# First expert block gathered by index, gate pieces moved around the turns, and separate waits in the expert tails

## The reference, cut to what matters

```python
x = x + parallel_mixer(rms_norm(x, g_mix), ...)
x = x + memory_cross_attention(rms_norm(x, g_xattn), rms_norm(mem, g_mem), ...)
x = x + hier_moe(rms_norm(x, g_moe), ...)              # expert width 512
x = rms_norm(x, g_final)
for l in range(2):
    x = _layernorm(alpha * x + _token_mixer(x, ...), ln1_g, ln1_b)    # alpha = 4 ** 0.25
    x = _layernorm(alpha * x + _hier_moe(x, ...), ln2_g, ln2_b)       # expert width 256

# hier_moe: top 1 of 4 groups by softmax, top 2 of its 8 experts
#   y = (silu(xb @ w_gate[e]) * (xb @ w_up[e])) @ w_down[e]
#   out[t] = sum of w * y over the token's two experts

# _token_mixer: z = x @ w_in, split in parts
y_a = _mla(...)                    # softmax attention
y_b = _stick_breaking(...)         # log sigmoid, suffix sums
y_c = _conformer_conv(...)
y_d = _forgetting_attention(...)   # logits + c[t] - c[s], c = cumsum(log_sigmoid(f))
gates = sigmoid(gate_logits + b_gate).reshape(b, s, 4, d)
merged = sum(einsum('bsnc,ncd->bsnd', ys, w_branch) * gates, axis=2)
return merged @ w_o
```

## Time and profile before

| | us |
|---|---|
| median of 3 runs | 2870.16 |
| lowest, highest | 2865.46, 2873.40 |
| the profiled execution | 2872.35 |
| span of its trace | 2870.5 |

### The profile page before, as it was taken

How to read it: one execution, slowest core, us unless ns; L and a number is a source line. 1 busy time by engine, 2 the same in 40 slices (tenths; PEclk the granted TensorE clock), 3 DMA queues, 4 the chain that set the end, 5 groups by cost and what they waited for, 6 DMA issues and landing times. The chain is left out here.

```text
span 2870.5 us, 50656 instructions
## 1 busy us (share of the span) xinstructions
PE 2500.0 (87%) x18285; PEld 1976.6 (69%) x18286; DVE 1364.5 (48%) x2996; ACT 926.8 (32%) x1739; POOL 363.6 (13%) x694
## 2 busy tenths in 40 slices
PE   7987799898888887999899889985989989989882
PEld 6976698764445446876677877764877767877662
DVE  6466335421111126735653744446744744654345
ACT  3534333221111114335442323324334633223222
POOL 1000000021212220000000034431000000014332
PEclk9998899699999998999999879997999989969997
DMA  4201325499999944132122579994222222469994
GB/s 150 74 1 60 103 89 208 174 408 405 409 405 412 395 199 164 45 83 56 47 64 61 201 278 365 386 374 144 78 64 56 56 55 79 179 240 386 375 390 159
DMA packets 209353, 565.32 MB, mean 197 GB/s; under 512 B 26768, under 2 KB 170768, under 8 KB 184640
## 3 DMA queue, kind: packets, MB, share of 16 engines
q1 hardware_dynamic: 191296, 538.74, 50.5%
q0 software_dynamic: 17920, 24.73, 2.6%
HBM read 559.69 MB, written 36.18 MB: 208 GB/s over the span
## 5 line engine op out<-in xcount | busy, mean ns | idle before, releaser
L989 PE MATMUL ps<-m_gate_up,e_xT 128*64 128x256 f32 x1088 | 270.7, 412 | 62.8 <-DMA m_gate_up<-in_w_gate_up 45.1
L989 PEld LDWEIGHTS ps<-r_gate_up,e_xT 128*64 128x64 f32 x2272 | 261.4, 142 | 86.9 <-issue 53.0
L989 PE MATMUL ps<-r_gate_up,e_xT 128*64 128x128 f32 x2272 | 273.5, 281 | 37.8 <-DMA r_gate_up<-in_w_exp_gate_up 24.8
L1159 DVE TENSOR_TENSOR e_hid<-e_silu,ps 64x128 f32<-64x128 f32 (+1 forms) x210 | 70.3, 335 | 473.6 <-ACT e_silu L1033 463.4
L989 PEld LDWEIGHTS ps<-m_gate_up,e_xT 128*64 128x64 f32 x1088 | 160.4, 149 | 175.2 <-issue 111.3
L1033 ACT ACTIVATE e_silu<-ps 64x128 f32<-64x128 f32 (+1 forms) x210 | 63.6, 303 | 660.0 <-PE ps L991 655.4
L991 PE MATMUL ps<-r_gate_up,e_xT 128*64 128x128 f32 x2272 | 273.7, 281 | 0.0
L991 PE MATMUL ps<-m_gate_up,e_xT 128*64 128x256 f32 x1088 | 270.7, 412 | 0.0
L991 PEld LDWEIGHTS ps<-r_gate_up,e_xT 128*64 128x64 f32 x2272 | 261.4, 142 | 0.0
L1242 POOL COPY e_tokcur<-e_tokcol 64x1 uint32 (+1 forms) x112 | 22.5, 201 | 1752.2 <-DVE e_tokcol L1119 1723.1
L2417 PE MATMUL ps<-t_hT,t1a_t1g_w 128*128 128x512 f32 x768 | 199.7, 411 | 4.8 <-PEq L54 2.4
(11 more groups left out here) (666 smaller groups left out, 4880.5 us busy)
## 6 DMA issues: line engine op xcount, KB each, us to landing
m_gate_up<-in_w_gate_up SPq DMA_DIRECT2D x32, 4096.0 KB
r_gate_up<-in_w_exp_gate_up SPq DMA_DIRECT2D x64, 2048.0 KB
m_down<-in_w_down SPq DMA_DIRECT2D x32, 2048.0 KB
r_down<-in_w_exp_down SPq DMA_DIRECT2D x64, 1024.0 KB
t0a_t0g_raw<-in_w_in SPq DMA_DIRECT2D x32, 512.0 KB, 3.8
t1a_t1g_raw<-in_w_in SPq DMA_DIRECT2D x32, 512.0 KB, 3.8
mixw_raw<-in_w_in SPq DMA_DIRECT2D x10, 1024.0 KB
xaw_raw<-in_w_kv_x SPq DMA_DIRECT2D x8, 1024.0 KB
```

The source lines that it names most:

```text
L989: nc.tensor.matmul(ps_gu[q][0:SLOTS], xT[:, c, :], ring.gu[s][:, 0, c, span], start=c == 0, stop=c == DC - 1)
L1159: vec.tensor_tensor(hid[SLOTS:P, q], silu[SLOTS:P, q], ps_gu[q][SLOTS:P], ALU.mult).then_inc(hid_ready, 1)
```

## The change

- **Expert stages.** The first block goes the way of the others: gather(0, 0), copy to `gathered`, `turn()`. The one-hot table and `first_rows` are gone. POOL clears `landing` with a memset. gather(2, 0) is issued only when DVE has copied block 0. DVE does all four `grow` ahead of the wait for block 0's rows. The number of full pairs joins the table; the counts of tokens have their own PSUM bank.
- **POOL's loop.** The index column of a store is copied before the wait for `y`, after a wait for the store two blocks back.
- **Tails.** DVE waits for the stores of the real blocks; SP does not wait for the store of e2's empty block. The norm's rows are loaded while the experts run. In e2's tail (x + mean) * gain is formed by DVE while ACT works on the root, and one more operation multiplies by the factor and adds the bias; ACT's rescale is gone there; the last tile is stored in two halves.
- **Gate pieces.** At u = 8, 16, 24 the projection (u, 2) and the half gate (u + 1, 0) change places; each of mx, sx, fx gets one half gate behind its transposes; the merged stage fs gets projection (16, 2). ma takes 26 pieces, sa 23, fa 22, `finish` 21.
- **fs, L2334, fr** become one stage; the log sigmoids are computed at the head of sa.

```diff
-def turn_split(nc, name, k, tiles, src, dst, n, factor=None):
+def turn_split(nc, name, k, tiles, src, dst, n, factor=None, pe_side=None):
...
                 turned.pe(pe)
+                if pe_side is not None:
+                    pe_side(pe)
...
+                if act_head is not None:
+                    act_head(act, link)
...
+                if norm.out is not None:
+                    read = sp.value_load(table[0:1, 1, (TURNS - 1) * RING + 2:(TURNS - 1) * RING + 3], min_val=1, max_val=MAX_BLOCKS)
+                    sp.wait_ge(gu_ready, read * 2)
+                    for n in range(2):
+                        sp.dma_start(norm_rows[:, n], norm.rows[n].partition_broadcast(P)).then_inc(norm_rows_landed, 16)
+                n_pairs, n_full = pairs_of_blocks(sp), full_pairs(sp)
+                sp.wait_ge(y_stored[1], n_full * 16 + 32)
+                sp.wait_ge(y_stored[0], n_pairs * 16 + 32)
...
-                    if norm.out is not None and t == 0:
-                        for n in range(2):
-                            sp.dma_start(norm_rows[:, n], norm.rows[n].partition_broadcast(P)).then_inc(norm_rows_landed, 16)
...
-                def first_rows():
-
-                    pe.wait_ge(first_pos_ready, 1)
-                    for c in range(DC):
-                        for t in range(TT):
-                            last = nc.tensor.matmul(ps_turn[:, c * SLOTS:(c + 1) * SLOTS], x[:, t, c * P:(c + 1) * P],
-                                                    first_pos[:, t, :], start=t == 0, stop=t == TT - 1)
-                    last.then_inc(turned, 1)
-
-                first_rows()
-                pe.wait_ge(table_ready, 2)
+                pe.wait_ge(rows_staged, 1)
+                turn()
...
-                nc.scalar.activation(landing[:].rearrange("p n d -> p (n d)"), k["ones"][0:SLOTS, 0:1].to_broadcast([SLOTS, 2 * D]),
-                                     ACT.Identity, scale=0.0).then_inc(landing_cleared, 1)
...
-                link(vec.tensor_scalar(near[:], in_block, 0.0, None, ALU.is_equal))
-                if not scaled:
-                    for j in range(2):
-                        last = vec.tensor_tensor(near[:, j * TT:(j + 1) * TT], near[:, j * TT:(j + 1) * TT], router.r[:, 2], ALU.mult)
-                    link(last)
-                link(vec.tensor_tensor(near_pos, at_pos.rearrange("p j t s -> p (j t) s"), cols(near[:], SLOTS), ALU.mult))
-                vec.tensor_tensor(first_pos, near_pos[:, 0:TT], near_pos[:, TT:], ALU.add).then_inc(first_pos_ready, 1)
...
-                    def grow(t):
-                        return vec.scalar_tensor_tensor(x[:, t, :], x[:, t, :], alpha, finish_rows[:, 0], ALU.mult, ALU.mult)
+                    dve.wait_ge(finish_landed, 32)
+                    for t in range(TT):
+                        last = vec.scalar_tensor_tensor(x[:, t, :], x[:, t, :], alpha, finish_rows[:, 0], ALU.mult, ALU.mult)
+                    link(last)
...
-                dve.sem_inc(rows_staged, 1)
+                dve.wait_ge(rows_gathered[0], 16)
+                vec.tensor_copy(gathered[:], landing[:, 0]).then_inc(rows_staged, 1)
                 turn_copy(1)
-                if finish is not None:
-                    dve.wait_ge(finish_landed, 32)
-                    for t in range(2):
-                        last = grow(t)
-                    link(last)
...
-                dve.wait_ge(choicecur_ready, g)
-                dve.wait_ge(y_stored[0], (g + 4) // 2 * 16)
-                dve.wait_ge(y_stored[1], (g + 3) // 2 * 16)
+                dve.wait_ge(y_stored[0], (g + 5) // 2 * 16)
+                dve.wait_ge(y_stored[1], (g + 4) // 2 * 16)
...
+                def shift(t):
+                    if norm.out is not None:
+                        if t == 0:
+                            dve.wait_ge(norm_rows_landed, 32)
+                        dve.wait_ge(centred, t + 1)
+                        vec.scalar_tensor_tensor(shifted[:, t, :], x[:, t, :], added[:, 1, t:t + 1], norm_rows[:, 0], ALU.add,
+                                                 ALU.mult).then_inc(grown, 1)
+
                 def last_factors(t):
                     if norm.out is not None:
-                        dve.wait_ge(normed, t + 1)
-                        if t == 0:
-                            dve.wait_ge(norm_rows_landed, 32)
-                        link(vec.tensor_tensor(x[:, t, :], x[:, t, :], norm_rows[:, 0], ALU.mult))
-                        vec.tensor_tensor(x[:, t, :], x[:, t, :], norm_rows[:, 1], ALU.add).then_inc(finished, 1)
+                        dve.wait_ge(grown, t + 1)
+                        form = (added[:, 4, t:t + 1], norm_rows[:, 1], ALU.mult, ALU.add)
+                        if t < TT - 1:
+                            vec.scalar_tensor_tensor(x[:, t, :], shifted[:, t, :], *form).then_inc(finished, 1)
+                        else:
+                            for h in range(2):
+                                at = slice(h * 512, (h + 1) * 512)
+                                vec.scalar_tensor_tensor(x[:, t, at], shifted[:, t, at], form[0], norm_rows[:, 1, at], ALU.mult,
+                                                         ALU.add).then_inc(half_finished, 1)
...
-                    for t in range(2, TT):
-                        last = grow(t)
-                    link(last)
...
                     pool.wait_ge(choicecur_ready, n + 1)
+                    pool.wait_ge(y_copied, n + 2)
                     step_aside()
...
+                nc.gpsimd.memset(landing[:], 0.0).then_inc(landing_cleared, 1)
                 pool.wait_ge(landing_cleared, 1)
                 pool.wait_ge(tokcol_ready, 1)
-                pool.sem_inc(tokcur_ready, 1)
-                gather(1, 1)
-                gather(2, 0)
-                nc.gpsimd.dma_start(spare_dram[4:5], ident[0:1, 0:SLOTS]).then_inc(rows_gathered[0], 16)
+                for n in range(2):
+                    gather(n, n)
                 for n in range(4):
                     nc.gpsimd.dma_start(spare_dram[n:n + 1], ident[0:1, 0:SLOTS]).then_inc(y_stored[n % 2], 16)
                 pool.wait_ge(choicecol_ready, 1)
+                pool.wait_ge(rows_staged, 1)
+                gather(2, 0)
...
-                        pool.wait_ge(y_copied, n + 2)
+                        pool.wait_ge(y_stored[p], pair * 16 + 32)
+                        step_aside(1)
...
+                        def _(pe):
+                            nc.tensor.matmul(sums, k["upto"][:], logs[:, 3], start=True, stop=False)
+                            for u in range(1, TT):
+                                last = nc.tensor.matmul(sums[:, u:TT], k["ones"][:], logs[:, 3, 0:TT - u],
+                                                        start=False, stop=u == TT - 1)
+                            last.then_inc(summed, 1)
+                            branches.pe_steps(pe, branches.next["pe"] + 1)
+                            pe.wait_ge(r_ready, 1)
+                            for j in range(4):
+                                for t in range(TT):
+                                    last = nc.tensor.matmul(ps[:, j, t * P:(t + 1) * P], r[:, t, j:j + 1].to_broadcast([P, P]),
+                                                            k["ident"][:], start=True, stop=True)
+                                last.then_inc(full, 1)
...
+        self.order = [(u, part) for u in range(self.units) for part in range(3)]
+        for u in range(DC, self.units, DC):
+            self.order[3 * u + 2:3 * u + 4] = [(u + 1, 0), (u, 2)]
...
-        return 3 * self.target + min(24, max(0, int((step + 1) * 24 / steps)))
+        span = 3 * self.target + 26 - self.start
+        return self.start + min(span, max(0, int((step + 1) * span / steps)))
...
-        turn_split(self.nc, name, self.k, TT, lambda t, c: ys[:, t, c * P:(c + 1) * P], self.yT, 2)
+        turn_split(self.nc, name, self.k, TT, lambda t, c: ys[:, t, c * P:(c + 1) * P], self.yT, 2,
+                   pe_side=lambda pe: self.pe_steps(pe, self.next["pe"] + 1))
```

202 lines of the change are left out of this document (87 added, 115 removed).

## The result

The changed kernel takes 2851.39 us (median of 6 runs, 2849.44 to 2858.35) beside 2869.19 for the one before (6 runs, 2863.6 to 2873.4) on the same chip: a ratio of 0.9949, interval 0.9934 to 0.9964. It is faster by 18 us, inside the range, but less than half of the 41 between 2870 and the 2829 that I gave as the likeliest. The profiled executions agree: 2852.16 (span 2849.7) against 2872.35 (2870.5).

A forecast was written before the change was run, and what follows sets the result against it. Bounds: PE in the attentions, standing DMA engines at the heads of e0 and e1, a chain in e2's tail. Heads, tails and mixers (-22) sum to -41.9 from 2872.35, less 2.2 to the median: 2829 us, range 2812 to 2852.

The forecast's parts named there:

- Heads: Start of the expert stages: gathering block 0 early gives -5.7 us in e0, -4.5 in e1, -0.3 in e2.
- A gather under full DMA load took 3.8 us: Heads: time from gather start to the copy waiting for it, read from an earlier row and used for block 0's landing.
- R3: Rival, heads: gather 0 queues behind the ring's loads, landing about 16 us late; 2867 us; chance 0.03, with R1 0.02.
- Each us by which the first expert is done earlier moves the whole stage: Heads of e0 and e1: the DMA engines stand until the first refill, so an earlier first expert shortens the stage equally.
- The memset ... Nothing: Heads: POOL's memset is done before `tokcol` comes, and the extra counting matmul falls on standing engines; 0 us.
- End of e2: Tail of e2: earlier read back and first add -6.2, with the stall and norm terms -8.3 us; bounds -5 and -11.
- stall -3.6, forms +1.7, half store -0.3: e2's tail behind the first add: second-tile stall goes, DVE's new norm forms cost 1.7 us, halved last store gives 0.3.
- Mixers: t0 and t1: -15.9 us each at full clock, about 0 at half clock in the turns; 0.7 of the way, -11 each.
- PE is the time there: Attentions: PE sets their length, so three half gates and one projection taken out gain all 10.8 us per mixer.
- R2: Rival, attentions: other waits come once PE's load falls, so only half of 10.8 is gained; 2840 us; chance 0.17.
- R1: Rival, mixer turns: clock stays low, gates take 4.9 us, mixers gain 0 instead of -11 each; 2851 us; chance 0.15.
- Merged fs: Each mixer, from sx's transposes to fa's first product: 15.7 us becomes 11.3 at full clock, -4.4.

The follow-up runs named there:

- h1: Changed kernel, but SP holds the ring's late loads in each expert stage until block 0's rows are staged; 2862.56 us in one execution.
- v1: Changed kernel, but only 2 of 8 MB of late loads in e0 and 4 of 10 in e1 go at once, the rest after block 0's rows; 2847.89 us.
- a1: Changed kernel, but ACT clears `landing` instead of POOL's memset, and the final norm has the earlier operations and whole stores; 2845.89 us in one execution.
- t1: As a run, not the mixer: changed kernel, but SP waits again for e2's empty block's store before reading back; 2856.15 us in one execution.
- h3: Changed kernel with the earlier head back: block 0 by one-hot matmuls, earlier order of gathers and grows, ACT clearing `landing`; 2850.57 us, ratio 0.9937.
- p1: Changed kernel with PE's half gates of units 9 to 16 cut from 12 matmuls to 4 (result wrong); sa takes 85.1 and 81.8 us.
- p2: Changed kernel with ACT's and DVE's gate operations of units 9 to 16 cut from 512 to 8 columns; sa 81.6 us, or 83.1 with a lower-clock stretch.
- m1: Changed kernel with the gate pieces back in their earlier order and places, merged fs and logs at sa's head kept; 2855.43 us, ratio 0.9950.
- s1: Changed kernel, but half gate (17, 0) moves from turn sx into sa, (17, 1) from fa into the turn, with a new count for weight splits; 2847.73 us.
- b1: Changed kernel with ACT clearing `landing`, late loads partly held in e0 and e1, (17, 0) in sa, no gate in sx, (17, 1) in fa; 2840.86 us.
- h2: Changed kernel, but block 1's gather is issued only when block 0's rows are staged; 2848.83 us.

## Why the prediction was right or wrong

- **Heads, forecast -10.5, measured +1.8: wrong, at the term for the landing.** "A gather under full DMA load took 3.8 us" was the step that failed, and it failed as a reading: the copy at 1846.84 waited for the gather of 1836.20, not for that of 1843.04, so the row of the kernel before showed 10.4. In the heads it took 10.1, 11.2 and 8.9, and 3.6 with the loads held (h1). With 10.4 in the sum for 3.8, 6.6 more, e0 would have come out at +0.9 and e1 at about +2, beside +0.8 and +1.7 measured. R3 had the right cause in the wrong form (a queue that lets the rows out last, 16 us and more); its condition, "a first gather of over 10 us", came true, at a chance that I had put at 0.05. The 6.3 and 7.4 us of landing that the sum lacked more than eat the gains of 5.7 and 4.5.
- **"Each us by which the first expert is done earlier moves the whole stage": false in e0, true in e1.** v1 had the refill 4.8 us earlier in e0 and none of it was left at the seventh. A stage that is all weight stream counts bytes and idle DMA time from its very start, not the time of the first refill; the idle slices of the earlier trace rows are a loss only if they are closed and not moved.
- **Grows ahead of the wait in e1**: they did end before the rows (at 1661.3). The block over all four grows, by which e1 would gain only 1, didn't come out: each delay ends with the one grow that runs (a1). e1 gained nothing for the other reason.
- **"The memset ... Nothing": wrong by 0.95 on DVE's path in each head** (a1). "The extra counting matmul" cost as well: the counting matmuls are 0.61 longer at half clock. Both lie in the path of the routing, +2.0 and +1.4; the remainder, 0.4 and 0.3, lies ahead of the counting matmuls, where the output projection's matmuls are 0.87 and 0.73 longer with more of them at the lower clock.
- **End of e2, forecast -8.3, measured -10.9: right in mechanism.** From the last down projection to the first add it fell from 15.4 to 9.2: the 6.2 of the forecast. The finer wait alone is 5.7 (t1). The 6.2 also needs that two grows have left the tail, which the sum took in silently with L1219 from 2828; with them back DVE is late by 2.4 (h3). The miss is all behind the first add: in place of "stall -3.6, forms +1.7, half store -0.3" that stretch fell from 31.9 to 27.3, and it is 27.3 with the old forms as well (a1), so the norm's rows loaded ahead gave 4.6 and the +1.7 was nothing.
- **Mixers, forecast -11 each, measured -6.8 and -6.3.** By thirds: ma and its turn grew by 5.5 and 7.5, by my terms 5.7 (a gate in the turn and its work). sa and its turn should have fallen by 7.5 and moved by +0.1 and -1.3. From fa to the last gate it fell by 12.4 and 12.5, by my terms 14.2. These terms are those of the full-clock sum, -15.9, from which 9.1 and 9.6 are missing: 7.5 and 6.2 of them in sa and its turn. So "PE is the time there" held in fa, the only attention whose row I read (83.00 of 83), down to the 76.5 that the change left it, and not in sa, where 0.8 of idle time hid a floor at about 82 (p1, p2). This is R2, at 0.17, with one attention in place of all: the pieces taken out are worth 4 to 6 us together (m1) instead of 12.
- **R1 came true in part**: half gates of 3.04 and 3.05 in mx of both and fx of t0, but 4.59 and 3.89 in sx and 4.03 in fx of t1, 3.4 us in all. The Trainium skill (TensorE: Matmul & The Clock Gate, HAM oscillation) says that bursts between long enough waits start cold each time; taken for every turn, as in the prediction, that put the mixers at 0, and measured are -6.8 and -6.3, with three of the six turns as it says. But the clock is not free of the change: behind the finish of t0 a stretch at the lower level lasts from 1570.2 to 1580.5, where before one lasted from 1582.2 to 1589.0.
- **Merged fs: right.** Forecast -4.4 from sx to fa with the gate, measured -3.1; without a gate in the turn -3.4 (m1).

Still open: whether s1's fa and finish grow by 1.9 and 1.5 from the new count for the splits or from the pieces' places, why one stretch at the lower clock opened inside sa of t0 (1403.0) and not of t1, and why b1's first gather in e0 stays at 10.0 with less on the way. None was tried by itself.

## What to carry to other kernels

Where a buffer has two halves, the row just before a wait is seldom the one that ends it: find in the code which half is waited for, and take the landing from the issue into that half. Before a gather is put at the head of a stage, look what loads are queued there, and hold back only as many as keep the engines busy while it lands. Taking work from an engine that is full pays down to the next floor, so read each stretch, and in it the idle time of the full engine and what its partners must do in turn, and not one stretch for all. In a stage that is a weight stream, an earlier start counts only if it closes idle time of the DMA engines.

## What the runs showed of the hardware

- The gather of a block of 64 places came in 3.6 us with nothing else in flight (44 rows of 4 KB, h1), and beside the loads in 9.9 with 44 rows, 11.45 with 64 and 8.3 with 14 (h2). What was left of the loads at the issue did not order these times: 4.3, 7.0 and 7.0 MB here, 0.6 MB for the 7.3 us of v1, 2.6 MB for the 10.0 of b1.
- The clock fell with the load: with PE's work in sa cut from 80.7 to 70.5 us the granted clock fell from 0.98 to 0.76 (p1), so the same matmuls took longer and a part of the cut came back.
- More work on PE made a stretch shorter: sa 84.8 to 83.3 in t1 with PE 79.1 to 81.4, both at full clock (s1). In t0 it is 86.8 to 83.3, of which 1.6 is a stretch at the lower clock that went.
- A small DVE operation beside a POOL memset ended with the memset, 1.13 instead of 0.18; beside one on ACT it didn't notice (a1).
